# The up product of a decoder layer with seven products in place of eight over half of its depth

## The reference, cut to what matters

```python
def hybrid_layer(x, ...):
    ...
    x = x + merged @ w_out
    f = rmsnorm(x, norm2_w) @ w_up            # (1088, 1024) @ (1024, 4096)
    x = x + jnp.square(jax.nn.relu(f)) @ w_down   # (1088, 4096) @ (4096, 1024)
    return x, new_conv, k, v
```

## Time and profile before

| | us |
|---|---|
| median of 3 runs | 1613.08 (1612.95 to 1613.3) |
| the profiled execution's own time | 1613.12 |
| its span, first to last instruction | 1611.4 |
| TensorE's mean granted clock | 0.999 |
| PE busy | 1600.1 (99%) |
| DVE busy | 1057.3 (66%) |
| POOL busy | 725.1 (45%) |
| ACT busy | 533.8 (33%) |

### The profile page before, as it was taken

How to read it: one execution, slowest core, us unless ns; L and a number is a source line. 1 busy time by engine, 2 the same in 40 slices (tenths; PEclk the granted TensorE clock), 3 DMA queues, 4 the chain that set the end, 5 groups by cost and what they waited for, 6 DMA issues and landing times.

```text
span 1611.4 us, 25421 instructions
## 1 busy us (share of the span) xinstructions
PE 1600.1 (99%) x9776; PEld 1482.7 (92%) x9776; DVE 1057.3 (66%) x1408; ACT 533.8 (33%) x1047; POOL 725.1 (45%) x597
## 2 busy tenths in 40 slices
PE   9999999999999999999999999999999999999998
PEld 8999999999998888999988989999999999999996
DVE  7685877859712221356433588777778888877777
ACT  6655665556522221432134411111111111111124
POOL 5212121121212111223587486666666776666653
PEclk9999999999999999999999999999999999999999
DMA  4201112011184767372354111110111111111012
GB/s 165 68 27 55 54 40 69 27 41 55 41 281 149 234 222 231 117 244 96 129 186 144 58 53 52 53 42 16 49 53 53 52 53 53 53 53 51 18 51 111
DMA packets 133491, 144.99 MB, mean 90 GB/s; under 512 B 7839, under 2 KB 98619, under 8 KB 133372
## 3 DMA queue, kind: packets, MB, share of 16 engines
q1 hardware_dynamic: 133226, 143.34, 27.8%
q10 hardware_dynamic: 146, 0.04, 0.0%
HBM read 124.37 MB, written 18.98 MB: 89 GB/s over the span
## 4 chain that ended last, share of the span: by engine, by line
PE 87%; DVE 8%; ACT 3%; issue 1%; DVEq 0%; ACTq 0%
PE ps L1307 51%; PE ps L1641 6%; PE ps L1642 6%; PE ps L1643 6%; DVE sp L2140 2%; PE ps L1598 2%; PE ps L1603 2%; PE ps L1601 2%; PE ps L1501 2%; DVE zc L2132 1%; PE ps L1457 1%; PE ps L1467 1%; PE ps L1545 1%; PE ps L1513 1%; ACT sp L1815 1%
## 5 line engine op out<-in xcount | busy, mean ns | idle before, releaser
L1307 PE MATMUL ps<-xh,wh 128*128 128x352 f32 (+1 forms) x956 | 322.3, 337 | 0.9 <-DVE xl L2113 0.7
L1307 PE MATMUL ps<-xh,wl 128*128 128x352 f32 (+1 forms) x956 | 312.5, 327 | 0.0
L1307 PE MATMUL ps<-xl,wh 128*128 128x352 f32 (+1 forms) x956 | 312.2, 327 | 0.0
L2269 DVE TENSOR_TENSOR x<-ps,x 128x1024 f32<-128x1024 f32 x210 | 257.1, 1225 | 42.9 <-PE ps L1643 24.5
L1150 POOL CAST wh<-raw 128x1024 fp32r<-128x1024 f32 x48 | 50.4, 1050 | 477.6 <-issue 213.2
L1307 PE MATMUL ps<-yh,wh 128*128 128x384 f32 (+1 forms) x768 | 250.5, 326 | 0.0
L1307 PE MATMUL ps<-yh,wl 128*128 128x384 f32 (+1 forms) x768 | 250.5, 326 | 0.0
L1307 PE MATMUL ps<-yl,wh 128*128 128x384 f32 (+1 forms) x768 | 250.2, 326 | 0.0
L1939 ACT ACTIVATE hf<-hf 128x384 f32<-128x384 f32 (+1 forms) x96 | 48.6, 508 | 554.9 <-DVE hf L2322 554.9
L1307 PEld LDWEIGHTS ps<-xh,wh 128*128 128x128 f32 x956 | 179.8, 188 | 17.2 <-issue 15.5
L1307 PEld LDWEIGHTS ps<-xl,wh 128*128 128x128 f32 x956 | 180.0, 188 | 0.7
(11 more groups left out here) (214 smaller groups left out, 3148.9 us busy)
## 6 DMA issues: line engine op xcount, KB each, us to landing
raw<-in_w_in SPq DMA_DIRECT2D x80, 256.0 KB, 3.3
cache<-in_cache_k SPq DMA_DIRECT2D x64, 256.0 KB, 3.8
cache<-in_cache_v SPq DMA_DIRECT2D x64, 256.0 KB, 3.6
raw<-in_w_up SPq DMA_DIRECT2D x64, 256.0 KB, 5.2
raw_d<-in_w_down SPq DMA_DIRECT2D x30, 512.0 KB, 4.1
raw<-in_w_out SPq DMA_DIRECT2D x48, 256.0 KB, 2.9
gates<-gst SPq DMA_DIRECT2D x16, 544.0 KB, 5.9
gb<-gates SPq DMA_DIRECT2D x16, 544.0 KB, 5.4
```

The lines of the kernel that those rows point to most:

```text
L1307: ins = mm(out, lhs[:, k * P:(k + 1) * P], rhs[:, x], start=(first and a == 0 and m == 0), stop=(last and a == n - 1 and m == 2))
L2269: V_.tensor_tensor(x, src, x, ALU.add).then_inc(step_free, 1)
```

## The change

From the second twin on (`n` = 1 to 15) the up product is a `mix`: over the first half of the depth (4 of 8 blocks) it is done by seven products in place of eight, the 2 x 2 cut being two blocks of depth by 512 rows on one side and two blocks of depth by one tile of the twin on the other; over the second half it stays plain. The 2 x 4 corners of the result need shared terms, so eight steps of PE (`MIX`, matmuls of 512 columns) gather in banks x, y, z and w. ACT copies the four stages of the sums that are wanted again into `hf` (`keep`), and a DVE addition joins bank and copy (`join`); ACT then does relu and square. The 64 sample rows are stationary (`y_few`, high and low side by side) with the weights moving beside them, copied out by ACT (`few_move`) and turned and summed by two matmuls against `both` (step 8). The row operands of the scheme are made once, behind the first twin: DVE keeps a plain copy `y_plain` (L2509), forms four differences (`twist`), ACT makes their high parts and DVE their low parts (`twist_low`).

The two weight rings become one of five places. Six entries a twin for the up product (four plain ones that are two blocks of depth for both tiles, two of two sums each: `up_op`) and eight for the down product (`down_op`) follow each other; a place goes to the next entry whose place is free first, and `slot_after` is the PE step that frees it. The first twin is computed as before, in pieces where its columns cross the borders of the new tiles of `y`. The four `sum` entries get two buffers in place of four, and the last two stand behind the `prep` that reads the buffer.

```diff
-            tail += [("sum", n - 1, k) for k in range(4)]
-            todo = list(PREP)
-            for m in range(6):
-                e = 2 * n + m // 3, m % 3
-                tail += [("up", *e), ("relu", *e)]
-                for _ in range(BESIDE_UP[m]):
-                    tail.append(("prep", n - 1, todo.pop(0)))
-            assert not todo
+            m = n - 1
+            tail += [("sum", m, 0), ("sum", m, 1), ("mix", n, 0), ("keep", n, 0), ("prep", m, 0), ("prep", m, "few0"), ("prep", m, "few1"),
+                     ("mix", n, 1), ("few_move", n), ("mix", n, 2), ("keep", n, 2), ("mix", n, 3), ("keep", n, 3), ("join", n, 1),
+                     ("prep", m, 1), ("prep", m, 6), ("mix", n, 4), ("mix", n, 8), ("mix", n, 5), ("keep", n, 5), ("prep", m, 3),
+                     ("prep", m, 4), ("join", n, 4), ("join", n, 8), ("sum", m, 2), ("prep", m, 2), ("sum", m, 3), ("mix", n, 6),
+                     ("join", n, 6), ("prep", m, 5), ("mix", n, 7), ("join", n, 7)]
...
+        MIX_BANK = {"x": 4, "y": 5, "z": 6, "w": 0, "few": 1}
+        MIX = [("x", 0, None), ("y", 1, (0, 0)), ("z", 3, None), ("x", 2, None), ("z", 5, (0, 1)), ("x", 4, None), ("w", 6, (1, 0)),
+               ("x", None, (1, 1))]
+        KEEP = {0: (0, 0), 2: (1, 1), 3: (0, 1), 5: (1, 0)}
+        JOIN = {1: (0, 0), 4: (0, 1), 6: (1, 0), 7: (1, 1)}
...
+        U_LAST = (1, 7, 7, 6, 3, 5)
...
-                return read_no["up", 2 * n + 3, 1]
+                return max(read_no["mix", n + 1, m] for m in (6, 8))
...
+        RING = []
+        for n in range(1, N_TWIN):
+            RING += [("u", n, x) for x in range(len(U_LAST))]
+            RING += [("d", n - 1, k) for k in range(N_OP)]
+        ring_no = {e: g for g, e in enumerate(RING)}
+
         def op_used(g):
 
-            n, k = divmod(g, N_OP)
-            return done_no[(OP_LAST[k][0], n, *OP_LAST[k][1:])]
+            kind, n, k = RING[g]
+            return done_no["mix", n, U_LAST[k]] if kind == "u" else done_no[(OP_LAST[k][0], n, *OP_LAST[k][1:])]
+
+        slot_of, slot_after = [], []
+        free_at = [tile_end["up", 0], tile_end["up", 0], tile_end["up", 1], tile_end["up", 1], tile_end["up", 1] + 1]
+        for g in range(len(RING)):
+            slot_of.append(free_at.index(min(free_at)))
+            slot_after.append(min(free_at))
+            free_at[slot_of[g]] = op_used(g)
+        TOP_FIRST = slot_of.index(N_RING - 1)
+        slot_after[TOP_FIRST] = tile_end["up", 1]
...
+            def slot_free(of):
+
+                pool.wait_ge(step_done, slot_after[of])
+                if of == TOP_FIRST:
+                    pool.wait_ge(twist_lo, 4)
...
+            def up_op(n, x):
+
+                rows_ = blocks(raw_u, 2 * P)
+                a11, a12, a21, a22 = (rows_[:, KQ * j:KQ * j + KQ, i * P:i * P + P] for i in range(2) for j in range(2))
+                s1, s2, s4, s3 = (blocks(tw[t])[:, KQ * h:KQ * h + KQ, :] for t in range(2) for h in range(2))
+                of = ring_no["u", n, x]
+                if x == 0:
+                    pool.wait_ge(u_in, 32 * n)
+                if x < 4:
+                    slot_free(of)
+                    split_op(of, raw_u[:, U_KT[x] * 2 * P:(U_KT[x] + 2) * 2 * P])
+                elif x == 4:
+                    twist(s1, a21, a22, ALU.add)
+                    twist(s2, s1, a11, ALU.subtract)
+                    slot_free(of)
+                    split_op(of, tw[0][:, :])
+                else:
+                    twist(s3, a11, a21, ALU.subtract)
+                    twist(s4, a12, s2, ALU.subtract)
+                    slot_free(of)
+                    split_op(of, tw[1][:, :])
...
+                for x in range(len(U_LAST)):
+                    up_op(n + 1, x)
+                for k in range(N_OP):
...
+                elif e[0] == "mix":
+                    _, n, m = e
+
+                    def three(out, w, y, start, stop):
+
+                        for t, (high, part) in enumerate(((0, 0), (0, 1), (1, 0))):
+                            ins = mm(out, w[high], y[part], start=start and t == 0, stop=stop and t == 2, skip_group_check=True)
+                        return ins
+
+                    def weight(x, at):
+
+                        slot = ring("u", n, x)
+                        return [t[:, at:at + P] for t in (w_hi_at[slot], w_lo_at[slot])]
+
+                    if m < len(MIX):
+                        where, p, over = MIX[m]
+                        out = bank(MIX_BANK[where])
+                        if m in (3, 4, 5, 7):
+                            pe.wait_ge(kept, 4 * (n - 1) + KEPT_FOR[m])
+                        else:
+                            pe.wait_ge(step_free, mix_bank_read(n, m))
+                        begun = where == "x" and m > 0 or (where == "z" and m > 2)
+                        if over:
+                            i, j = over
+                            for f in range(KT // 2, KT):
+                                x, at = PLAIN_AT[f]
+                                pe.wait_ge(d_lo, ring_no["u", n, x] + 1)
+                                ins = three(out, weight(x, at + i * P), [y_at(f, part, j * HS, (j + 1) * HS) for part in range(2)],
+                                            not begun and f == KT // 2, p is None and f == KT - 1)
+                            begun = True
...
+                        if p is not None:
+                            pe.wait_ge(d_lo, ring_no["u", n, W_AT[p][0][0]] + 1)
+                            if n == 1 and p in TWIST_NO:
+                                pe.wait_ge(twist_lo, TWIST_NO[p] + 1)
+                            for q in range(KQ):
+                                ins = three(out, weight(*W_AT[p][q]), [y_op[p][part][:, q * HS:(q + 1) * HS] for part in range(2)],
+                                            not begun and q == 0, q == KQ - 1)
...
+                elif e[0] == "few_move":
+                    n = e[1]
+                    act.wait_ge(step_done, done_no["mix", n, 1])
+                    if n >= 2:
+                        act.wait_ge(step_done, done_no["mix", n - 1, 8])
+                    A(few_rows[:, :], bank(MIX_BANK["few"], 0, 2 * P), ACT.Copy).then_inc(few_moved, 1)
+                elif e[0] == "keep":
+                    _, n, m = e
+                    i, j = KEEP[m]
+                    if n >= 2 and m == 0:
+                        act.wait_ge(op_lo, len(PREP) * (n - 1))
+                    act.wait_ge(step_done, done_no["mix", n, m])
+                    A(hf[n % 2][i][:, j * HS:(j + 1) * HS], bank(MIX_BANK[MIX[m][0]]), ACT.Copy).then_inc(kept, 1)
+                elif e[0] == "join":
+                    _, n, m = e
+                    act.wait_ge(step_free, read_no["mix", n, m])
+                    parts = [hf[n % 2][JOIN[m][0]][:, JOIN[m][1] * HS:(JOIN[m][1] + 1) * HS]] if m < 8 else [hf[n % 2][i][:, SEQ:NTOK] for i in range(2)]
+                    for x in parts:
+                        if m < 8:
+                            A(x, x, ACT.Relu).then_inc(relu_made, 1)
+                            act.wait_ge(relu_made, 4 * (n - 1) + RELU_NO[m])
+                        A(x, x, ACT.Square).then_inc(hf_made, 1)
...
+                        if f < KT // 2 and b < NB:
+                            x = (f % KQ) * HS + b * P % HS
+                            V_.tensor_scalar(y_plain[f // KQ, b * P // HS][:, x:x + P], src, w2c[:, f:f + 1], None, ALU.mult)
...
+                elif e[0] == "join":
+                    _, n, m = e
+                    v.wait_ge(step_done, done_no["mix", n, m])
+                    if m < 8:
+                        i, j = JOIN[m]
+                        x = hf[n % 2][i][:, j * HS:(j + 1) * HS]
+                        v.wait_ge(kept, 4 * (n - 1) + 1 + [KEEP[k] for k in (0, 2, 3, 5)].index(JOIN[m]))
+                        V_.tensor_tensor(x, bank(MIX_BANK[MIX[m][0]]), x, ALU.add).then_inc(step_free, 1)
+                    else:
+                        if n >= 2:
+                            v.wait_ge(op_hi, len(PREP) * (n - 1))
+                        for i in range(2):
+                            ins = V_.tensor_scalar(hf[n % 2][i][:, SEQ:NTOK], bank(MIX_BANK["few"], 2 * P + i * SMP, 2 * P + (i + 1) * SMP),
+                                                   0.0, None, ALU.max)
+                        ins.then_inc(step_free, 1)
...
                     if k == 2:
+                        v.wait_ge(op_hi, prep_no[n, 3] + 1)
                         v.wait_ge(sum_made, 4 * n + 1)
                     elif k == 3:
+                        v.wait_ge(op_hi, prep_no[n, 2] + 1)
                         v.wait_ge(sum_made, 4 * n + 3)
                     one, op, other = ((low[0], ALU.add, low[1]), (top[0], ALU.subtract, low[0]),
-                                      (sums_[0][:, :], ALU.subtract, top[0]), (top[1], ALU.subtract, sums_[2][:, :]))[k]
-                    V_.tensor_tensor(sums_[k][:, :], one, other, op).then_inc(sum_made, 1)
```

(4 more changed lines are left out.)

275 lines of the change are left out of this document (179 added, 96 removed).

## The result

| | before | changed |
|---|---|---|
| median of the runs | 1613.08 us | 1714.46 us (1712.49 to 1715.93, 4 runs) |
| span of the profiled execution | 1611.4 us | 1712.0 us |
| ratio | | 1.0628, 95% interval 1.0609 to 1.0646 |

The changed kernel is 6.3% slower.

The account below looks back on a forecast made before the run. PE's own matmuls were taken to set the time. Work 43.67 plus waits 3.7, 1.05 and 1.6 made a 50.0 us cycle, +81.2 over 15; with once-costs, +86.6 on 1613.12 gave 1700 us, range 1632 to 1722.

Parts of the forecast that it names:

- if the clock falls in the cycles: Sign named beforehand: the prediction would be wrong if TensorE's granted clock dropped within the cycles.
- PE's work: PE's matmuls in one cycle: 43.67 us without waits, 0.94 less than before.
- wait before p0: Before the down product's first step, PE waits for join 6 from 6.82 to 10.5 us behind m5: 3.7 us.
- wait before p1's second half: In the down product's second step, PE waits for DVE's last addition of p0: another 1.05 us a cycle.
- ring: At the cycle's head, PE waits in m1 and m2 for POOL's weight entries: 1.6 us, between 0.2 and 2.2.
- TensorE's clock: Rival: PE's idling halves the clock and each p0 runs at 1.2 GHz, +2.7 a cycle, 1741 us; 7%.
- once, in all: Costs outside the repeated cycle, in first twin, first cycle and last cycle: 2.0 + 0.4 + 1.0 + 2.0 us.
- Join of DVE and ACT: Behind m5, DVE's SBUF operations take turns with POOL; join 6 ends at 10.47 us, giving waits of 3.7 and 1.05.
- The pieces: First twin's passes cut into smaller matmuls: 2.0 us for the two tiles, between 1 and 5.
- The 2.0 for `end_low`: In the last cycle `end_low` waits for join 7, delaying d7: 2.0 us, between nothing and 3.
- faster: Rival: join 6 ends before PE needs it at 6.82, leaving only PE's 43.67 us a cycle: 1602 us; 8%.
- DVE slips between POOL's instructions: Rival: waits at their lower bounds, 0.5 + 1.05 + 0.2, cycle 45.4 us, 1631 us, up to 1650; 14%.

Follow-up runs that it names:

- e8: The changed kernel with DVE's and ACT's order rearranged, five of POOL's high-part copies a cycle on ACT, and the first twin and last cycle mended: 1612.85 us.
- e1: The changed kernel with 14 more matmuls of 512 columns in front of the wait before each cycle's first down product: 1697.01 us.
- e2: The changed kernel with POOL held at down entry 1 until join 6 has read its bank: 1726.09 us.
- e4: The changed kernel with joins 6 and 7 ahead of sums 2 and 3 and low parts 2 and 5, these spread over the first down products: 1637.78 us.
- e5: e4 with sums 0 and 1, low part 0 and the small copy's low parts moved from the cycle's head to around and behind join 1: 1625.4 us.
- e6: e5 with ACT making the high parts of five ring entries a cycle in POOL's place: 1616.26 us.
- e9: The kernel before, with only the first twin's up product cut at columns 512 and 1024 as the changed kernel cuts it: 1618.47 us.

## Why the prediction was right, and where its sum was short

Direction, size and the mechanism of the main wait were right. One of its own signs of being wrong came too: "if the clock falls in the cycles". By its own steps (us a cycle):

| step | forecast | measured | from |
|---|---|---|---|
| PE's work | 43.67 | 43.94 | cycle of e8 |
| wait before p0 | 3.7 | 3.57 late at 1299.30, and in 14 of 15 | timeline |
| wait before p1's second half | 1.05 | 1.14 and 0.7 in the 2 cycles where the clock stays | timeline |
| ring | 1.6 | 0.8 (0.64 of wait at 1331.32, and the restarts) | timeline |
| TensorE's clock | 0 | 2.7 in 11 cycles, less in 2 | windows, e1 |
| cycle | 50.0 | 50.7 | p0 at 947.66 and at 1657.60, 14 cycles |
| once, in all | 5.4 | 9 to 10 | rest of the 101.4 us |

- *PE's work.* Right within 0.3. m8 itself was 0.39 for the 0.4 taken; most of the 0.3 lies in the first 512-column matmuls behind the sample rows' of 256 (24 + 16 + 30 + 4 + 36 matmuls of a mix took 5.44, 1.89, 7.06, 0.39 and 8.26 us, and 30 at 0.227 are 6.82).
- *Join of DVE and ACT.* The hand layout put join 6's end 10.47 behind m5 and PE's wait at 3.7; it was 10.2 and 3.4. The wait is shown by the trace, and its cause by e2 (wait gone with POOL held) and e4 (wait gone with the sums elsewhere). Each restart behind a wait costs 0.1 more than the wait (0.31 us between the first two matmuls in place of 0.227), which no step had.
- *Second wait.* Right in size, but it needs a p0 at full speed. In 13 cycles the slow clock hid it.
- *Ring.* Half of the forecast. The prediction's own terms, 8.5 and five turns of 0.33, come to 10.1 and a wait of 1.9, not 9.9 and 1.6. DVE took fewer turns from POOL there than the five reckoned with: in e4's cycle three POOL instructions at the head were longer, by 0.85 together (the text of e5 has them). e5 and e6 show that POOL's length of work was the limit, as supposed.
- *The clock.* The step that failed is the weight given to a rival. The prediction saw the granted clock of 0.72 at the end of the span, took the rival's price rightly as 2.7 a cycle, and gave it 7%. It happened in 13 of 15 cycles, and was worth 17.4 us (e1). In the sum the clock stood at nothing. The rival's time of 1741 was too high, because it kept the second wait beside the slow p0, and took the ring at 1.6.
- *Once.* The pieces were 5.0 and not 2.0 (e9): the upper end, which was named, was the truth. By its own line the 72 pieces more would even have been 1.0, 0.013 each. The last relu of the first twin, which stood on DVE behind the low parts of the twisted rows, held PE 2.7 us at m0 of the first cycle: this was in no step; the text had put the operand differences "beside" the last two passes without laying DVE's order out there. Behind that wait the granted clock was 0.50 for 3.3 us, some 1.4 us more. With the pieces and the 2.7 that is 9.1. The 2.0 for `end_low` in the last cycle did not come: PE waited for no d7 there.
- *Two errors in the cycle nearly cancelled*: 0.8 too much for the ring and 1 for the second wait, against some 2.2 for the clock (its mean over the 15) and 0.3 for PE's work. That the total came within 14 us is in part luck: the clock, which the sum left out, and two terms that were too large made up for each other.

The rival that had PE's fewer matmuls win ("faster", 1602) was right about what it hung on: with DVE and POOL out of the way the cycle is 43.94. It was wrong about the total, because the once-costs at the two ends (5.0 for pieces, some 2.5 for the start of the first mix, 1.9 in the last cycle) eat nearly all of the 10 us. That DVE slips between POOL's instructions, as another rival had it, happened in one cycle of 15, the one with the wait of 1.73.
